# Sums of squares added over chunks on VectorE, and x's norm taken between the memory's keys

## What is computed

```python
def rms_norm(x, g):
    y = x * lax.rsqrt(jnp.mean(x * x, axis=-1, keepdims=True) + EPS)
    return y * g

h  = rms_norm(x, norm1_g)              # into every projection of the layer
mn = rms_norm(mem, mem_norm_g)         # mem is (256, 2048)
k, v = jnp.split(mn @ w_mem_kv, 2, axis=-1)     # 4 heads of 128 each
k = rms_norm(k.reshape(B, N_MEM, 4, 128), xk_g)
```

## Time and profile before

| | us |
|---|---|
| median of 3 runs | 4055.09 (4050.82 to 4055.88) |
| profiled execution | 4051.33 |
| its span | 4048.9 |
| TensorE busy | 3897.9 (96%) |
| VectorE busy | 2270.1 (56%) |
| ScalarE busy | 1208.3 (30%) |
| GpSimd busy | 1426.5 (35%) |

### The profile page before, as it was taken

One profiled execution on the slowest core, in us unless ns is written; L12 is line 12 of the kernel. 1 busy time (PEld: TensorE's weight loads), 2 busy tenths in 40 slices (PEclk: granted clock), 3 DMA queues, 4 the chain that ended last, 5 costly groups with the idle time before them and its releaser, 6 DMA issues.

```text
span 4048.9 us, 54432 instructions
## 1 busy us (share of the span) xinstructions
PE 3897.9 (96%) x20187; PEld 3552.6 (88%) x20187; DVE 2270.1 (56%) x3187; ACT 1208.3 (30%) x1392; POOL 1426.5 (35%) x1090
## 2 busy tenths in 40 slices
PE   8999978999999898998889999999999999999999
PEld 5777855888888786888889999999999999999999
DVE  4273153000000205888995777777777767776776
ACT  3333343333333223223552222222222222222221
POOL 0434423444444564444223333233322222222211
PEclk9999989999999999999999999999999999999999
DMA  4322201222222322323447888888878888888786
GB/s 170 109 73 93 104 31 37 98 93 95 101 93 94 134 91 88 109 101 112 188 186 290 321 313 327 312 314 324 326 290 292 300 317 296 303 299 308 279 305 224
DMA packets 165744, 804.19 MB, mean 199 GB/s; under 512 B 15504, under 2 KB 79000, under 8 KB 79512
## 3 DMA queue, kind: packets, MB, share of 16 engines
q1 hardware_dynamic: 124608, 530.62, 36.0%
q0 software_dynamic: 36864, 268.45, 18.2%
q10 hardware_dynamic: 4184, 4.01, 0.5%
HBM read 746.92 MB, written 56.10 MB: 198 GB/s over the span
## 4 chain that ended last, share of the span: by engine, by line
PE 77%; DVE 12%; issue 7%; DMA 2%; ACT 1%; POOL 1%; DVEq 0%; POOLq 0%; SPq 0%; ACTq 0%
PE bank L1439 76%; DVE ohB L1311 2%; DVE arena L1243 1%; DMA ring<-w_exp 1%; DVE arena L1240 1%; DVE arena L1247 1%; DVE w_lo L1328 1%; POOL p_lo L564 1%; DVE arena L1258 1%; DVE g_acc L1362 0%; DVE arena L1270 0%; DVE h_lo L1194 0%; DMA act_in<-gelus 0%; ACT w_hi L660 0%; DVE smax L1157 0%
## 5 line engine op out<-in xcount | busy, mean ns | idle before, releaser
L564 POOL TENSOR_TENSOR p_lo<-ring,p_hi 128x512 fp32r<-128x512 f32 x464 | 613.8, 1324 | 776.3 <-ACT p_hi L660 776.3
L1439 PE MATMUL bank<-h_hi,w_hi 128*128 128x384 f32 (+1 forms) x2304 | 793.0, 344 | 14.5 <-DVE h_lo L1224 14.5
L1439 PE MATMUL bank<-h_lo,w_hi 128*128 128x384 f32 (+1 forms) x2304 | 785.9, 341 | 0.0
L1439 PE MATMUL bank<-h_hi,w_lo 128*128 128x384 f32 (+1 forms) x2304 | 785.7, 341 | 0.0
L660 ACT ACTIVATE w_hi<-ring 128x2048 fp32r<-128x2048 f32 x272 | 520.9, 1915 | 830.4 <-PE bank L1439 778.1
L1439 PE MATMUL bank<-act_hi,w_hi 128*128 128x384 f32 x2048 | 686.9, 335 | 11.6 <-DVE w_lo L1328 11.6
L1439 PE MATMUL bank<-act_lo,w_hi 128*128 128x384 f32 x2048 | 685.9, 335 | 0.0
L1439 PE MATMUL bank<-act_hi,w_lo 128*128 128x384 f32 x2048 | 685.8, 335 | 0.0
L1328 DVE TENSOR_TENSOR w_lo<-ring,w_hi 128x2048 fp32r<-128x2048 f32 x224 | 515.2, 2300 | 229.5 <-ACT w_hi L660 229.4
L660 ACT ACTIVATE p_hi<-ring 128x512 fp32r<-128x512 f32 x464 | 293.6, 634 | 873.7 <-PE bank L1439 860.2
L1439 PE MATMUL bank<-norm_hi,p_hi 128*128 128x512 f32 x1216 | 485.0, 399 | 10.7 <-POOL p_lo L564 9.6
(11 more groups left out here) (176 smaller groups left out, 5087.7 us busy)
## 6 DMA issues: line engine op xcount, KB each, us to landing
ring<-w_exp SPq DMA_DIRECT2D x256, 1024.0 KB
ring<-w_mix SPq DMA_DIRECT2D x64, 1024.0 KB, 4.8
gelus<-gel SPq DMA_DIRECT2D x128, 192.0 KB
tables<-wt SPq DMA_DIRECT2D x12, 2048.0 KB, 6.4
wg<-tables SPq DMA_DIRECT2D x16, 1536.0 KB, 13.6
act_in<-gelus SPq DMA_DIRECT2D x16, 1536.0 KB
ring<-w_qk SPq DMA_DIRECT2D x20, 1024.0 KB, 4.8
ring<-w_o SPq DMA_DIRECT2D x16, 1024.0 KB, 4.8
```

Source lines behind the costliest of these rows:

```text
L564: nc.gpsimd.tensor_tensor(p_lo[:, part, :], ring[slot][:, part, :], p_hi[:, part, :].bitcast(F32), ALU.subtract).then_inc(quarter_lo, 1)
L1439: return nc.tensor.matmul(out, lhsT, rhs, start=start, stop=stop)
```

## The change

The squares of the memory are added on VectorE: the quarters 1, 2 and 3 (4 chunks each, 128 x 1024) are added one by one onto quarter 0, each add after ScalarE's square of that quarter and after the add before it. TensorE then makes 4 ones products in place of 16. The same is done for x (quarters of 128 x 2048), on VectorE behind the memory's scaling and the two small steps and ahead of the head norms. TensorE's 4 products for x move from behind the third head's sum to behind the first head's sum. x's root moves on ScalarE to behind the second head's root, its reciprocal on VectorE to behind the second head's norm, and both use a buffer of their own, `rtx`. The wait for all head norms ahead of x's root is gone. The helper `step` on VectorE is only defined earlier.

```diff
--- before.py
+++ after.py
@@ -225,6 +225,7 @@
         branch_hi = [mix_hi[k // 12][:, k % 12, :] for k in range(KC)]
         branch_lo = [mix_lo[w][:, k, :] for w, n in enumerate((HA, LC, HC)) for k in range(n)]
 
+        rtx = at(Z + 2048, S)
         sumsq = at(Z, S)
         sqx = at(Z + 512, S)
         rt2 = at(Z + 1024, S)
@@ -261,6 +262,7 @@
         mem_in, x_in, vec_in = [sem(f"mem_in{i}") for i in range(4)], [sem(f"x_in{i}") for i in range(4)], sem("vec_in")
         const_made = sem("const_made")
         mem_sq, x_sq = sem("mem_sq"), sem("x_sq")
+        mem_acc, x_acc = sem("mem_acc"), sem("x_acc")
         norm_ss = sem("norm_ss")
         norm_rt = sem("norm_rt")
         mem_h, h_ready = sem("mem_h"), sem("h_ready")
@@ -698,9 +700,9 @@
                 if k == 0:
                     act_e.wait_ge(mem_h, KC)
                 head_root(k, MEM, k + 1)
-            act_e.wait_ge(norm_ss, 2)
-            act_e.wait_ge(head_ok, HC)
-            f(rt[0], bank[6][:, :], ACT.Sqrt, scale=1.0 / D, bias=eps[:, 0:1]).then_inc(norm_rt, 1)
+                if k == 1:
+                    act_e.wait_ge(norm_ss, 2)
+                    f(rtx, bank[6][:, :], ACT.Sqrt, scale=1.0 / D, bias=eps[:, 0:1]).then_inc(norm_rt, 1)
 
             for c in range(KC):
                 act_e.wait_ge(h_made, c + 1)
@@ -990,9 +992,19 @@
             v = nc.vector
             st = Steps(dve, dve_step)
 
+            def step(ins):
+                st.did(ins)
+                st.wait()
+
             v.memset(ones[:, :], 1.0).then_inc(const_made, 1)
             v.memset(eps[:, :], EPS).then_inc(const_made, 1)
 
+
+            for q in range(1, 4):
+                dve.wait_ge(mem_sq, q + 1)
+                if q > 1:
+                    dve.wait_ge(mem_acc, q - 1)
+                v.tensor_tensor(msq[:, 0:4, :], msq[:, 0:4, :], msq[:, 4 * q:4 * q + 4, :], ALU.add).then_inc(mem_acc, 1)
 
             dve.wait_ge(vec_in, 16 * 6)
             dve.wait_ge(norm_rt, 1)
@@ -1020,17 +1032,22 @@
                 v.scalar_tensor_tensor(out=dst, in0=dst, scalar=gain, in1=r, op0=ALU.mult, op1=ALU.mult
                                        ).then_inc(head_ok, 1)
 
+            for q in range(1, 4):
+                dve.wait_ge(x_sq, q + 1)
+                if q > 1:
+                    dve.wait_ge(x_acc, q - 1)
+                v.tensor_tensor(xsq[:, 0:4, :], xsq[:, 0:4, :], xsq[:, 4 * q:4 * q + 4, :], ALU.add).then_inc(x_acc, 1)
+
             for k in range(HC):
                 head_norm(k, mk[:, k, :], MEM, hgain[:, 3:4], k + 1)
-
-
-            dve.wait_ge(norm_rt, 2)
-            st.did(v.reciprocal(rt[0], rt[0]))
-            st.wait()
+                if k == 1:
+                    dve.wait_ge(norm_rt, 2)
+                    step(v.reciprocal(rtx, rtx))
+
             for c in range(KC + 1):
                 if c < KC:
                     v.scalar_tensor_tensor(out=hT[:, c, :], in0=xT[:, c, :], scalar=vecs[:, c:c + 1],
-                                           in1=rt[0], op0=ALU.mult, op1=ALU.mult).then_inc(h_made, 1)
+                                           in1=rtx, op0=ALU.mult, op1=ALU.mult).then_inc(h_made, 1)
                 if c:
 
                     dve.wait_ge(h_high, c)
@@ -1040,10 +1057,6 @@
 
             dve.wait_ge(lam_exp, 1)
             y, z, z2, s4 = sp[:, 1, :], sp[:, 2, :], sp[:, 3, :], sp[:, 4, :]
-
-            def step(ins):
-                st.did(ins)
-                st.wait()
 
             step(v.tensor_scalar(z, y, 2.0, None, ALU.add))
             step(v.reciprocal(z, z))
@@ -1451,9 +1464,9 @@
                 mm(bank[4 + n % 2][:, 0:width], ones[:, :], sq[n % 2][:, 0:width]).then_inc(head_ss, 1)
 
             pe.wait_ge(const_made, 4)
-            for c in range(KC):
-                pe.wait_ge(mem_sq, c // 4 + 1)
-                ins = mm(bank[6][:, 0:MEM], ones[:, :], msq[:, c, :], start=(c == 0), stop=(c == KC - 1))
+            pe.wait_ge(mem_acc, 3)
+            for c in range(4):
+                ins = mm(bank[6][:, 0:MEM], ones[:, :], msq[:, c, :], start=(c == 0), stop=(c == 3))
             ins.then_inc(norm_ss, 1)
             landed(pe, T_MK)
             for c in range(KC):
@@ -1467,11 +1480,13 @@
                     if k >= 3:
                         pe.wait_ge(head_rt, k - 2)
                     head_sum(k - 1, MEM, k)
-
-            for c in range(KC):
-                pe.wait_ge(x_sq, c // 4 + 1)
-                ins = mm(bank[6][:, :], ones[:, :], xsq[:, c, :], start=(c == 0), stop=(c == KC - 1))
-            ins.then_inc(norm_ss, 1)
+                if k == 1:
+                    pe.wait_ge(x_acc, 3)
+                    pe.wait_ge(norm_rt, 1)
+                    for c in range(4):
+                        ins = mm(bank[6][:, :], ones[:, :], xsq[:, c, :], start=(c == 0), stop=(c == 3))
+                    ins.then_inc(norm_ss, 1)
+
             pe.wait_ge(head_rt, HC - 2)
             head_sum(HC - 1, MEM, HC)
```

## The result

| | runs | median, us | lowest to highest |
|---|---|---|---|
| before | 4 | 4052.95 | 4049.78 to 4055.88 |
| after | 4 | 4087.42 | 4082.48 to 4095.17 |

The ratio is 1.0089, with a 95% interval of 1.0077 to 1.0102: the change made the kernel slower, by 34.5 us of the medians. The forecast was 4044.5 us, in a range from 4038 to 4052. The profiled execution took 4088.44 us.

A forecast was written before the change was run, and what follows sets the result against it. The prediction took TensorE to bound the kernel (77% of the chain's span). Gains of 0.8 us from memory's norm and 8.9 from the key heads' stretch made 9.7 us off, forecast 4044.5 us, range 4038 to 4052.

The forecast's parts named there:

- TensorE's return: TensorE resuming after its wait behind the V products: forecast at 89.3 us in place of 98.97, 9.7 us earlier.
- Memory's norm: Start of the kernel: three VectorE adds, then eight TensorE instructions from 14.6 us; table load near 18.3, gain 0.8 us.
- x's product: TensorE's ones products for x: 8 of 32 instructions remain, 3.43 us, behind the first head sum; 10.3 us removed.
- The bare wait: TensorE's last key head sum, now right behind head sum 3, waits for block 4's square: 1.4 us idle, V 2.27 after T.
- The adds of x: Three VectorE adds, 7.0 us, ending at 35.6 with 3.0 us margin before TensorE needs the sum; costed at nothing.
- V ended last: Before TensorE resumes: the V products end at 86.1 us, 3.5 us behind the loop that makes h.
- Sum. 0.8 + 8.9 = 9.7 us off: Total gain: 0.8 us from memory's norm and 8.9 from the key heads' stretch, taken off the whole run.
- The slower side: Rival: VectorE's adds of x stretched further, at 8 us per add 4.3 us slower than before; chance 0.02.
- stretched adds on VectorE: Rival: adds of x at 5.5 us each stall TensorE 6.6 us, gain 3.1, about 4051; chance 0.08.
- The clock: Rival: TensorE's clock takes 3.4 us of the gain, about 4048, chance 0.15; or gives, about 4041, chance 0.08.
- If the stage behind 89 us has lost what came ahead of it: Sign that the forecast is wrong: the time gained before TensorE resumes near 89.3 us is lost again afterwards.
- The chance of 0.02 for slower: Chance that the whole run is slower, made up only of adds of x stretched beyond the point where the gain is eaten.

The follow-up runs named there:

- after_pad95: The changed kernel with 95 instructions that only wait on a semaphore already reached, ahead of TensorE's first product: 4041.54 us, ratio 0.9974 to the kernel before.
- after_pad25: The changed kernel with 25 instructions that only wait, ahead of TensorE's first product: 4122.58 us, one run.
- before_pad161: The kernel before, unchanged but for 161 instructions that only wait, ahead of TensorE's first product: 4102.48 us, ratio 1.0129.
- after_pad256: The changed kernel with 256 instructions that only wait, ahead of TensorE's first product: 4105.37 us, ratio 1.0124 to the kernel before.

## Why the prediction was wrong

**Local terms.** The stretch up to TensorE's return was right in mechanism and nearly in size: 9.07 us for 9.7. Memory's norm was put at 0.8 and gave 0.3 (table load at 18.79 against 19.06): the squares began 0.16 us later, the three adds took 3.89 and TensorE started 0.15 behind them, at 14.95 for 14.6; its eight instructions took the long pace, as was said (3.75 us with the tail). x's product measured 42.53 - 38.66 - 0.43 = 3.44 us for 3.43. The bare wait ran from 56.77 to V at 59.14, 2.37 us for 2.27, with 1.26 us idle in it. The adds of x, put at nothing, cost nothing: 7.07 us for 7.0, with the margin of 3.0 us. V ended last, by 3.7 us for 3.5.

**The step that failed** is "Sum. 0.8 + 8.9 = 9.7 us off". It took for granted that all behind TensorE's return keeps its length. The runs show that it does only if the instructions keep their place: with the place restored the sum holds (11.6 us by the medians of after_pad95, with an interval of 6 to 15 for a forecast of 9.7), and with it lost the expert loop takes 46 us more: TensorE fetches the loop's code again at each of eleven jumps. The change was counted in microseconds of work removed and not in instructions of program removed. The numbers that raise the question (95 fewer ahead of a loop of 1586) could be had from the diff and the trace of the kernel before. They don't say that the new place is a bad one; that took runs.

**The rivals.** The slower side was given to stretched adds on VectorE; they ran at 2.29 us each and had no part in it. The clock did take part, but in the expert loop, behind gaps of 2.8 us on average (the expectations say 3.2, the one gap that had been looked at), and not in V. "If the stage behind 89 us has lost what came ahead of it" was the sign named for this outcome, without a mechanism. The chance of 0.02 for slower had no part for this: 49 of 256 places are bad for this loop, so an edit that moves it by a number nobody looked at meets one about once in five.

**What stays open.** Why a loop that touches eight blocks is not kept is not settled. Nor is why 9 packets a turn (and not 8) come; one block fetched ahead beyond the loop's eight would be 9. The share of the clock was worked out from the traces, and no run tried it by itself.

## What to carry to other kernels

When an engine's long loop is not unrolled, count its instructions and how many the edit adds or takes ahead of it, and read the instruction queues' packets in both profiles before the edit is judged. A cost that recurs once a turn, is put down to "issue" and lies at the loop's jump was code fetched again here, and the packets on the instruction queue are the test; a few dozen waits in idle time at the start (here 50, hidden while TensorE waits for the first sums) moved the loop off the bad place. To judge an edit, compare at equal place: here the same edit measured 1.0089 and 0.9974.

## What the runs showed of the hardware

- TensorE ran a loop of 1586 instructions from 2320 to 3500 us, over eight turns, with no packet on its instruction queue (before), and at other places of the same loop fetched 9 packets of 16.4 KB for every jump back, with a gap of 2.2 to 3.4 us at the jump (after), or two gaps a turn, 44.8 us in 22 (after_pad25).
- Places 256 instructions apart did the same: after (-95) against before_pad161 and after_pad256 (both +161), with 147, 148 and 148 packets.
- An instruction that waits on a semaphore already reached cost TensorE 0.11 us (161 of them: 18.98 us to the first product).
